# Dilated attention: probabilities turned in 32x32 squares by VectorE and placed by ScalarE

## The reference

```python
s = jnp.einsum('nbqhe,nbkhe->nbhqk', qb, kw) * (1.0 / math.sqrt(E))
s = jnp.where(valid, s - slopes * dist * dil, -jnp.inf)
m = jnp.max(s, axis=-1, keepdims=True)
e = jnp.exp(s - m)
p = e / jnp.sum(e, axis=-1, keepdims=True)
o = jnp.einsum('nbhqk,nbkhe->nbqhe', p, vw)
```

## Time and profile before

| | |
|---|---|
| median of 3 runs | 3137.13 us (3136.91 to 3138.24) |
| profiled execution, its own time | 3137.17 us |
| its span | 3135.3 us |
| PE busy in the span | 3117.0 us (99%) |
| DVE busy | 2015.0 us (64%) |
| ACT busy | 1908.9 us (61%) |
| mean granted clock of PE | 0.999 of the full 2.4 GHz |

### The profile page before, as it was taken

The page is one execution under the profiler, slowest core; times in us unless marked ns, Lnnn a source line. Parts: engine busy times, 40 slices in busy tenths (PEclk is TensorE's granted clock), DMA queues, the critical chain, the costliest instruction groups (busy, mean ns, idle before and its releaser), DMA issues.

```text
span 3135.3 us, 41268 instructions
## 1 busy us (share of the span) xinstructions
PE 3117.0 (99%) x15124; PEld 2632.7 (84%) x15124; DVE 2015.0 (64%) x1803; ACT 1908.9 (61%) x2592; POOL 442.4 (14%) x562
## 2 busy tenths in 40 slices
PE   9999999999999999999999999999999999999998
PEld 9988888888888888888888888879988888888887
DVE  6776665566565555567655656577876676666767
ACT  5457677667766556557555455556565865666655
POOL 2112443344352000000000000003330000000000
PEclk9999999999999999999999999999999999999999
DMA  8556555565546544546555555545445555545553
GB/s 315 188 192 222 210 209 206 204 217 211 197 175 230 192 162 170 191 161 252 190 187 201 189 198 189 187 148 225 154 185 182 208 184 204 197 175 202 184 206 119
DMA packets 116214, 612.97 MB, mean 196 GB/s; under 512 B 11040, under 2 KB 39840, under 8 KB 46624
## 3 DMA queue, kind: packets, MB, share of 16 engines
q1 hardware_dynamic: 93824, 597.62, 51.9%
q10 hardware_dynamic: 22304, 14.16, 1.5%
HBM read 599.16 MB, written 12.58 MB: 195 GB/s over the span
## 4 chain that ended last, share of the span: by engine, by line
PE 96%; DVE 2%; ACT 1%; DMA 1%; issue 0%; SPq 0%; ACTq 0%; DVEq 0%
PE ps L2513 28%; PE ps L2515 28%; PE ps L2514 28%; PE ps L2376 2%; PE ps L2378 2%; PE ps L2377 2%; PE ps L2413 1%; PE ps L2406 1%; PE ps L2400 1%; DMA raw<-weights 1%; DVE wlo L1323 1%; PE ps L2586 0%; PE ps L2835 0%; PE ps L2538 0%; PE ps L2729 0%; PE ps L2710 0%
## 5 line engine op out<-in xcount | busy, mean ns | idle before, releaser
L1323 DVE TENSOR_TENSOR wlo<-raw,whi 128x2048 fp32r<-128x2048 f32 x540 | 1232.8, 2293 | 802.9 <-ACT whi L618 799.7
L618 ACT ACTIVATE whi<-raw 128x2048 fp32r<-128x2048 f32 x540 | 1017.7, 1899 | 900.8 <-PE ps L2515 815.3
L2513 PE MATMUL ps<-whi,x_pair 128*128 128x512 f32 x2304 | 898.9, 390 | 0.0
L2515 PE MATMUL ps<-whi,x_pair 128*128 128x512 f32 x2304 | 896.5, 389 | 0.0
L2514 PE MATMUL ps<-wlo,x_pair 128*128 128x512 f32 x2304 | 896.4, 389 | 0.0
L2515 PEld LDWEIGHTS ps<-whi,x_pair 128*128 128x128 f32 x2304 | 432.4, 188 | 90.0
L2514 PEld LDWEIGHTS ps<-wlo,x_pair 128*128 128x128 f32 x2304 | 432.5, 188 | 89.5
L2513 PEld LDWEIGHTS ps<-whi,x_pair 128*128 128x128 f32 x2304 | 432.5, 188 | 89.4
L2513 PE MATMUL ps<-whi,hid_hi 128*128 128x512 f32 x1280 | 499.3, 390 | 0.0
L2514 PE MATMUL ps<-wlo,hid_hi 128*128 128x512 f32 x1280 | 498.0, 389 | 0.0
L2515 PE MATMUL ps<-whi,hid_lo 128*128 128x512 f32 x1280 | 498.0, 389 | 0.0
(11 more groups left out here) (400 smaller groups left out, 3239.3 us busy)
## 6 DMA issues: line engine op xcount, KB each, us to landing
raw<-weights SPq DMA_DIRECT2D x537, 1024.0 KB, 4.8
read_tab<-read_tables SPq DMA_DIRECT2D x2, 3072.0 KB, 10.4
read_tables<-c_wide ACTq DMA_DIRECT2D x32, 128.0 KB, 1.9
drive_tables<-drive_out ACTq DMA_DIRECT2D x16, 256.0 KB, 3.7
drive_tab<-drive_tables SPq DMA_DIRECT2D x4, 1024.0 KB, 9.4
raw<-weights SPq DMA_DIRECT2D x4, 640.0 KB, 11.9
x_in<-x_t SPq DMA_DIRECT2D x4, 512.0 KB, 8.8
raw<-weights SPq DMA_DIRECT2D x8, 256.0 KB, 9.7
```

What stands on the lines that cost most here:

```text
L618: act.activation(whi[:, s, 0:width], raw[:, s, 0:width], ACT.Copy).then_inc(hi_ready, 1)
L1323: dve.tensor_tensor(wlo[:, s, 0:width], raw[:, s, 0:width], whi[:, s, 0:width].bitcast(F32), ALU.subtract).then_inc(lo_ready, 1)
L2513: pe.matmul(o, xh[:, k, t], whi[:, s, c], start=first and j == 0, stop=False)
L2515: ins = pe.matmul(o, xl[:, k, t], whi[:, s, c], start=False, stop=last and j == 3)
```

## The change

Seven heads, all but the last (h = 7), are no longer turned by PE. `score` and `prob_t` become a pair, `heads_buf`, whose roles alternate: head h has its scores and probabilities in `heads_buf[h % 2]`. DVE transposes that buffer in 32x32 squares into the other one (`turn_probs`), and ACT copies the squares back to their places in the head's own buffer with 16 activations over 32 partitions (`place_probs`); `mix(h)` reads them there. Head 7 keeps PE's `turn` and `copy_turned`. New waits: `shift(h)` waits for `turned_copied` of head h - 1 and `turn_probs(h)` for `head_done` of head h - 1, since these write the buffer that was read there; `scores(h)` waits for `shift_ready` of head h - 1 instead of `turned_copied`.

The order is written anew around them: on PE `mix(h)` and `mix(h + 1)` of the first two heads stand two slots and one slot later, and the mix of the third head stands ahead of slot 0 of the block that follows (or ahead of the output projection).

```diff
+            def place_probs(h):
+                act.wait_ge(prob_turned, h + 1)
+                squares, dst = heads_buf[1 - h % 2], heads_buf[h % 2]
+                for i in range(4):
+                    for j in range(4):
+                        part = squares[32 * i:32 * i + 32].rearrange("p g (b q c) -> p q (g b) c", q=4, c=32)[:, j]
+                        to = dst[32 * j:32 * j + 32].rearrange("p g (b i c) -> p i (g b) c", i=4, c=32)[:, i]
+                        ins = act.activation(to, part, ACT.Copy)
+                ins.then_inc(turned_copied, 1)
...
@@ ACT, four_heads(k)
                 exps(h)
                 hi1(q + 4, 2)
                 move_qk(b + 3)
-                copy_turned(h)
                 hi1(q + 4, 3)
-                hi1(q + 5, 0)
+                place_probs(h)
+                hi_part(q + 5, 0, 2)
+                exps(h + 1)
                 copy_head(h)
-                hi1(q + 5, 1)
-                exps(h + 1)
                 hi1(q + 5, 2)
                 copy_v(b + 4)
                 hi1(q + 5, 3)
-                copy_turned(h + 1)
+                place_probs(h + 1)
...
                 move_qk(b + 7)
-                copy_turned(h + 2)
                 hi1(q + 8, 3)
+                place_probs(h + 2)
                 hi_part(q + 9, 0, 2)
                 exps(h + 3)
                 hi1(q + 9, 2)
@@ DVE, shift(h)
                 dve.wait_ge(scores_done, h + 1)
+                own = heads_buf[h % 2]
+                if h:
+                    dve.wait_ge(turned_copied, h)
...
+            def turn_probs(h):
+                dve.wait_ge(prob_ready, h + 1)
+                if h:
+                    dve.wait_ge(head_done, h)
+                own, squares = heads_buf[h % 2], heads_buf[1 - h % 2]
+                dve.transpose(squares[:].rearrange("p g c -> p (g c)"), own[:].rearrange("p g c -> p (g c)")).then_inc(prob_turned, 1)
...
@@ DVE, four_heads(k)
                 probs(h + 2)
+                turn_probs(h + 2)
                 turn_qk(b + 7)
                 lo_part(q + 8, 2, 4)
-                lo_part(q + 9, 0, 2)
+                lo1(q + 9, 0)
                 shift(h + 3)
+                lo1(q + 9, 1)
                 probs(h + 3)
@@ PE, scores(h)
                 if h:
-                    pe.wait_ge(turned_copied, h)
+                    pe.wait_ge(shift_ready, h)
@@ PE, four_heads(k)
                 if k:
-                    attn_slots(b, 0, 1)
                     mix(h - 2)
-                    turn(h - 1)
-                    attn_slots(b, 1, 3)
+                    attn_slots(b, 0, 3)
                     mix(h - 1)
...
                 attn_slots(b + 3, 2, 4)
-                attn_slots(b + 4, 0, 1)
-                turn(h)
-                attn_slots(b + 4, 1, 2)
-                mix(h)
+                attn_slots(b + 4, 0, 2)
                 scores(h + 1)
                 attn_slots(b + 4, 2, 4)
-                attn_slots(b + 5, 0, 1)
-                turn(h + 1)
-                attn_slots(b + 5, 1, 2)
+                mix(h)
+                attn_slots(b + 5, 0, 3)
                 mix(h + 1)
-                attn_slots(b + 5, 2, 4)
+                attn_slots(b + 5, 3, 4)
...
                 scores(h + 2)
                 attn_slots(b + 7, 2, 4)
-                attn_slots(b + 8, 0, 1)
-                turn(h + 2)
-                attn_slots(b + 8, 1, 2)
+                attn_slots(b + 8, 0, 2)
                 scores(h + 3)
                 attn_slots(b + 8, 2, 4)
@@ PE, output projection
+            mix(N_HEADS - 2)
             chunk(q, 0)
             pe.wait_ge(qk_turned, 2 * len(PAIRED))
             head_rows(0, 0, 0, low)
-            mix(N_HEADS - 2)
             turn(N_HEADS - 1)
```

More of the change, by code:

```diff
@@ L260, in build @@
         qk_turns = at("qk_turns", 86, [P, 2, 512])
+        heads_buf = (score, prob_t)
         dist = at("dist", 73.5, [P, N_GROUPS, 384])
@@ L367, in build @@
         scores_done, shift_ready, exp_done, prob_ready = sem("scores_done"), sem("shift_ready"), sem("exp_done"), sem("prob_ready")
-        turned, turned_copied, head_done, head_hi, head_lo = (sem(n) for n in ("turned", "turned_copied", "head_done", "head_hi", "head_lo"))
+        prob_turned, turned, turned_copied, head_done, head_hi, head_lo = (
+            sem(n) for n in ("prob_turned", "turned", "turned_copied", "head_done", "head_hi", "head_lo"))
         compact_landed, skip_landed, job_ready, job_turned, job_lags, job_copied, lags_copied, inner_ready, reads_stored, drive_stored, inner_stored = (
@@ L927, in move_qk @@
                 ins.then_inc(qk_moved, 1)
+            def place_probs(h):
[7 more added lines that the diff above has]
+                ins.then_inc(turned_copied, 1)
             def copy_turned(h):
-                act.wait_ge(turned, h + 1)
-                act.activation(prob_t[:], ps[:, 4:7, 0:384], ACT.Copy).then_inc(turned_copied, 1)
+                act.wait_ge(turned, 1)
+                act.activation(heads_buf[1 - h % 2][:], ps[:, 4:7, 0:384], ACT.Copy).then_inc(turned_copied, 1)
             def copy_head(h):
@@ L938, in exps @@
                 act.wait_ge(shift_ready, h + 1)
-                act.activation(score[:, :, 0:128], score[:, :, 0:128], ACT.Exp, bias=row_max[:, 0:1], scale=ATTN_SCALE,
+                own = heads_buf[h % 2]
+                act.activation(own[:, :, 0:128], own[:, :, 0:128], ACT.Exp, bias=row_max[:, 0:1], scale=ATTN_SCALE,
                                accum_out=row_den[:, 0:1])
-                act.activation(score[:, :, 128:384], score[:, :, 128:384], ACT.Exp, bias=row_max[:, 1:2], scale=ATTN_SCALE,
+                act.activation(own[:, :, 128:384], own[:, :, 128:384], ACT.Exp, bias=row_max[:, 1:2], scale=ATTN_SCALE,
                                accum_out=row_den[:, 1:2]).then_inc(exp_done, 1)
@@ L960, in four_heads @@
                     hi1(q, 3)
-                    hi1(q + 1, 0)
                     copy_head(h - 2)
-                    copy_turned(h - 1)
-                    hi_part(q + 1, 1, 3)
+                    place_probs(h - 1)
+                    hi_part(q + 1, 0, 3)
                     copy_head(h - 1)
@@ L1768, in shift @@
                 dve.wait_ge(scores_done, h + 1)
+                own = heads_buf[h % 2]
+                if h:
+                    dve.wait_ge(turned_copied, h)
                 for g in range(N_GROUPS):
                     step(dve.scalar_tensor_tensor(
-                        out=score[:, g, :], in0=dist[:, g, :],
+                        out=own[:, g, :], in0=dist[:, g, :],
                         scalar=const[:, bass.ds(h + (CONST["slope"] + g * N_HEADS), 1)],
@@ L1774, in shift @@
                 step.settle()
-                step(dve.tensor_reduce(row_max[:, 0:1], score[:, :, 0:128], AX.XY, ALU.max))
-                step(dve.tensor_reduce(row_max[:, 1:2], score[:, :, 128:384], AX.XY, ALU.max))
+                step(dve.tensor_reduce(row_max[:, 0:1], own[:, :, 0:128], AX.XY, ALU.max))
+                step(dve.tensor_reduce(row_max[:, 1:2], own[:, :, 128:384], AX.XY, ALU.max))
                 step.settle()
@@ L1782, in probs @@
                 dve.wait_ge(exp_done, h + 1)
+                own = heads_buf[h % 2]
                 step(dve.reciprocal(row_den[:], row_den[:]))
                 step.settle()
-                dve.tensor_scalar(score[:, :, 0:128], score[:, :, 0:128], row_den[:, 0:1], None, ALU.mult)
-                dve.tensor_scalar(score[:, :, 128:384], score[:, :, 128:384], row_den[:, 1:2], None, ALU.mult).then_inc(prob_ready, 1)
+                dve.tensor_scalar(own[:, :, 0:128], own[:, :, 0:128], row_den[:, 0:1], None, ALU.mult)
+                dve.tensor_scalar(own[:, :, 128:384], own[:, :, 128:384], row_den[:, 1:2], None, ALU.mult).then_inc(prob_ready, 1)
+            def turn_probs(h):
[4 more added lines that the diff above has]
+                dve.transpose(squares[:].rearrange("p g c -> p (g c)"), own[:].rearrange("p g c -> p (g c)")).then_inc(prob_turned, 1)
             def head_low(h):
@@ L1813, in four_heads @@
                     lo1(q, 3)
-                    lo1(q + 1, 0)
                     head_low(h - 2)
-                    lo_part(q + 1, 1, 3)
+                    turn_probs(h - 1)
+                    lo_part(q + 1, 0, 3)
                     head_low(h - 1)
@@ L1837, in four_heads @@
                 probs(h)
+                turn_probs(h)
                 turn_qk(b + 3)
@@ L1840, in four_heads @@
                 lo1(q + 5, 0)
+                shift(h + 1)
+                lo1(q + 5, 1)
+                probs(h + 1)
                 head_low(h)
-                lo1(q + 5, 1)
-                shift(h + 1)
-                probs(h + 1)
+                turn_probs(h + 1)
                 lo_part(q + 5, 2, 4)
@@ L2716, in turn @@
                     for b in range(3):
-                        ins = pe.transpose(ps[:, 4 + g, b * P:(b + 1) * P], score[:, g, b * P:(b + 1) * P], ccol("ident"))
```

(6 more changed lines are left out.)

## The result

The changed kernel takes **3146.07 us** (median of 9 runs, 3144.74 to 3147.71) against 3137.13 us (9 runs, 3136.43 to 3138.24) on the same chip: the ratio is 1.0029 with a 95% interval of 1.002 to 1.0037. It is slower by 8.9 us. The profiled execution of it took 3145.95 us, its span is 3143.6 us.

The account below looks back on a forecast made before the run. PE's own instructions were taken to bound the kernel. To the profiled 3137.17 us it added - 6.93 (turns) + 12.2 (two stalls) + 3.2 (lower clock) = + 8.5, giving 3145.6 us, range 3141.9 to 3150.1.

Parts of the forecast that it names:

- PE's turns: On PE in the attention blocks: seven of eight turns go, 0.99 us each, 6.93 us off a stream without gaps.
- The prices of the new operations: Per head: DVE's 128x1152 transpose 1.37 us; ACT's sixteen 32x288 activations 442 ns each alone, 7.26 us together.
- The walk to the copy of V: Queues followed to ACT's copy of V, ending 1145.05: PE waits 6.1 us at the mixes of heads 2 and 6, 12.2 together.
- the full gain: Case with the copy of V hidden as well: the whole - 6.93 us, 3130.2 us; chance 0.04.
- The cover of the weight slots: PE's waits for DVE's low parts: the ring of four slots covers one placing of 7.26 us, so costed at nothing.
- The clock: Term for PE's lower clock level after the two stalls: 2 x 1.6 = 3.2 us added.
- The clock behind the stall: Step claiming both stalls, longer than 4.25 us, drop PE's granted clock once each: 1.6 us apiece.
- rival 1: Both stalls at the mixes occur but PE's clock stays up in one or both: 3142.4 to 3144 us; chance 0.20.
- rival 3: ACT reaches the copy of V in time, PE waits 1.1 us at each mix, clock holds: 3132.4 us; chance 0.07.

Follow-up runs that it names:

- late mix with early shift: Changed kernel with PE's mixes of heads 2 and 6 back where they stood before and DVE's fourth-head shift ahead of the low part: 3130.17 us.
- the turns alone: Kernel before without PE's nine transposes for each of heads 0 to 6, waits and order otherwise kept: 3129.54 us, ratio 0.9977.
- half of the placing: Changed kernel without 8 of the 16 placing activations of each head: 3137.32 us, ratio 0.9999.

## Why the prediction was right

I had said 3145.6 us, within 3141.9 to 3150.1, and slower with 0.79. Its steps, against the profiled execution:

- **PE's turns.** 6.93 us predicted. 7.0 to 7.1 in the traces (late mix with early shift, and the turns alone), 6.9 to 7.4 by the medians: 1.0 us a turn, as the earlier trace rows had it.
- **The prices of the new operations.** The 32x288 activation has a median of 442 ns over its 112 instances, the estimate to the nanosecond, and sixteen occupy 7.22 us (7.26). The transpose takes 1369 or 1379 ns (1370). Interpolating from the nearest forms in the earlier trace rows was good enough.
- **The walk to the copy of V.** Each step fell within 0.6 us: shift of head 2 at 1107.70 (1107.95), end of the placing at 1132.6 (1133.1), end of block 8 at 1138.84 (1139.1), end of the copy at 1144.5 (1145.05). The stall came out at 5.8 us instead of 6.1, two of them 11.5 instead of 12.2. The named cause holds too: take DVE's low part from ahead of the shift and 3.9 us of the stall go. So does what the rivals named as the way to the full gain: with a step between block and mix again and ACT in time, 3130.17 came out, where they had 3130.2.
- **The cover of the weight slots.** Costed at nothing; no wait of PE for a low part appears in the attention stage of the change.
- **The clock.** 3.2 us predicted, 3.8 measured (2.3 and 1.5): one stretch was twice as long as the other, but of its time part lay inside the wait. That each fall cost about 1.6 was in part luck: the figure came from PE's pace at the start of the trace, where the record shows a granted clock of 1.00, and in the other execution of the change the two cost 2.8 and 1.7.

The two errors, - 0.7 in the stalls and + 0.6 in the clock, cancel by luck. Summed: - 7.1 + 11.5 + 3.8 = + 8.2, where the trace has + 8.6 from the first `scores` to PE's last matmul; 0.4 us are in no term.

One step was right by its number but wrong in its reason: **"The clock behind the stall"**. I read from the earlier trace rows that the clock fell 4.25 us after the last matmul and argued that both stalls are longer than that. Kernels with waits of 2.0, 2.3 and 2.9 us had it fall as well. So the ground given for rival 1, that 6.1 is not far above 4.25, was no ground: 4.25 us is what one fall showed, not what it takes. The remark in rival 3, that behind a gap of 1.1 us the clock holds, was borne out at 1.2 and 1.7 us; carried over to 2 us, as I did for half of the placing, it was false.

## What to carry to other kernels

Work taken off a full engine pays only if what it is handed to is not late at the next place where the full engine waits: here 7 us were gained on PE, and more than that was lost to a copy at the end of ACT's queue. Before a consumer is moved up to its producer, walk the producer's queue, with the new work in it, to the very instruction that the consumer waits for; and when a helper engine gets longer steps, move what others wait for ahead of what has room. Where PE must wait for some microseconds anyway, count the slower matmuls behind the wait too, or give PE something to do.

## What the runs showed of the hardware

The granted clock fell behind waits that I had thought too short for it. Waits of PE at the mixes, and the granted clock behind them: 5.6 us (twice in each of two executions), 0.50; 2.9, 2.3 and 2.0 us, 0.50; 1.7 us (twice) and 1.2 us (twice), 1.00. All but the first are from one profiled execution each, and the spread of the runs with half of the placing speaks for a fall that does not come every time. How long the stretch at 0.50 lasts is not fixed by the wait either: at the second wait of the change it was twice as long in one execution as in the other. Behind the waits of 2.0 and 2.9 us the lower level began only after PE had resumed, so a profile shows the slow matmuls apart from the wait that they follow: the first row of the mix is at full pace (0.91 us) and the second is not (2.54 and 2.20 us, against 1.50). Filling the wait with matmuls that nobody needs took the fall away both times that it was tried, at no cost to the mix behind them.
